# Recurrent scan of the second layer: first level on the keys themselves, sixteen-wide cells and the last distance moved to ScalarE

## What is computed

```python
log_f = jnp.logaddexp(jnp.log(lb), jnp.log1p(-lb) + jax.nn.log_sigmoid(f))
k = (1.0 - lb) * jax.nn.sigmoid(-f)
# per chunk, G = cumsum(log_f):
attn  = einsum('bhtk,bhsk,bhtsk->bhts', q, k, exp(G_t - G_s))   # s <= t
o     = einsum('bhts,bhsv->bhtv', attn, v) + einsum(q * exp(G), state)
```

## Time and profile before

| | us |
|---|---|
| median of 3 runs | 1880.17 |
| lowest, highest | 1879.79, 1880.75 |
| the profiled execution's own time | 1879.63 |
| its span in the profile | 1877.8 |
| PE busy | 1840.6 (98%) |
| DVE busy | 1147.7 (61%) |
| ACT busy | 938.7 (50%) |
| POOL busy | 588.5 (31%) |

### The profile page before, as it was taken

One profiled execution on the slowest core, in us unless ns is written; L12 is line 12 of the kernel. 1 busy time (PEld: TensorE's weight loads), 2 busy tenths in 40 slices (PEclk: granted clock), 3 DMA queues, 4 the chain that ended last, 5 costly groups with the idle time before them and its releaser, 6 DMA issues.

```text
span 1877.8 us, 25493 instructions
## 1 busy us (share of the span) xinstructions
PE 1840.6 (98%) x10128; PEld 1588.0 (85%) x10128; DVE 1147.7 (61%) x2028; ACT 938.7 (50%) x1107; POOL 588.5 (31%) x131
## 2 busy tenths in 40 slices
PE   8899999999998999999999999999999999999998
PEld 7688888888897988888888888899888889888887
DVE  7788878776888787222776322567522287862227
ACT  7455555455653554444554544453444455544443
POOL 2000000000000003888100888400588800058880
PEclk9899999999999999999999999999999999999999
DMA  9344444454243335655543555544655543365551
GB/s 360 112 159 156 143 164 152 180 196 155 93 166 131 120 128 195 215 191 192 187 181 136 181 194 189 188 190 165 227 199 192 190 177 135 112 233 199 193 190 65
DMA packets 53049, 325.56 MB, mean 173 GB/s; under 512 B 8624, under 2 KB 11056, under 8 KB 15568
## 3 DMA queue, kind: packets, MB, share of 16 engines
q1 hardware_dynamic: 45328, 310.49, 45.2%
q10 hardware_dynamic: 7616, 13.59, 2.1%
HBM read 323.02 MB, written 1.05 MB: 173 GB/s over the span
## 4 chain that ended last, share of the span: by engine, by line
PE 85%; DVE 10%; issue 2%; ACT 2%; DMA 1%; DVEq 0%; ACTq 0%
PE project L1102 31%; PE output L1102 31%; PE turn L1500 5%; PE project L1500 5%; PE project L1506 2%; PE turn L1506 2%; PE turn L1323 2%; DVE wlo L1962 2%; PE output L1288 1%; PE output L1263 1%; DVE arena L2302 1%; DMA raw<-in_units 1%; DVE arena L2079 1%; DVE arena L2325 1%; PE turn L1242 1%
## 5 line engine op out<-in xcount | busy, mean ns | idle before, releaser
L1059 POOL TENSOR_TENSOR wlo<-raw,whi 128x2048 fp32r<-128x2048 f32 x127 | 588.3, 4664 | 1240.8 <-ACT whi L1569 1224.1
L1569 ACT ACTIVATE whi<-raw 128x2048 fp32r<-128x2048 f32 x289 | 547.0, 1910 | 342.6 <-PE project L1500 166.2
L1102 PE MATMUL project<-whi,XT 128*128 128x512 f32 x1376 | 453.3, 400 | 11.4 <-ACT arena L1578 9.0
L1962 DVE TENSOR_TENSOR wlo<-raw,whi 128x2048 fp32r<-128x2048 f32 x162 | 368.3, 2285 | 23.1 <-ACT whi L1569 20.0
L1102 PEld LDWEIGHTS project<-whi,XT 128*128 128x128 f32 x1376 | 259.7, 189 | 67.0 <-ACT arena L1578 8.2
L1102 PE MATMUL output<-whi,YTh 128*128 128x512 f32 x736 | 288.1, 392 | 1.5 <-DVE YTl L2456 1.5
L1102 PE MATMUL output<-whi,YTl 128*128 128x512 f32 x736 | 287.1, 390 | 0.0
L1102 PE MATMUL output<-wlo,YTh 128*128 128x512 f32 x736 | 286.9, 390 | 0.0
L2740 DVE TENSOR_TENSOR arena<-project,arena 128x256 f32<-128x256 f32 x48 | 20.4, 425 | 409.1 <-ACT arena L1918 409.1
L1102 PE MATMUL project<-wlo,XT 128*128 128x512 f32 x688 | 268.9, 391 | 0.0
L1102 PE MATMUL project<-XT,whi 128*128 128x256 f32 x1184 | 219.0, 285 | 0.1
(11 more groups left out here) (283 smaller groups left out, 2386.8 us busy)
## 6 DMA issues: line engine op xcount, KB each, us to landing
raw<-in_units SPq DMA_DIRECT2D x290, 1024.0 KB, 4.8
arena<-in_ln_g ACTq DMA_DIRECT2D x8, 512.0 KB, 5.4
arena<-in_ln_b ACTq DMA_DIRECT2D x8, 512.0 KB, 7.3
raw<-in_units SPq DMA_DIRECT2D x2, 512.0 KB, 7.3
tok<-in_mem SPq DMA_DIRECT2D x1, 1024.0 KB, 14.4
arena<-in_x_t SPq DMA_DIRECT2D x1, 1024.0 KB, 18.2
xres<-in_x SPq DMA_DIRECT2D x1, 1024.0 KB, 20.1
arena<-in_mem_t ACTq DMA_DIRECT2D x1, 1024.0 KB, 4.5
```

The costliest lines, as they stand in the source:

```text
L1059: pool.tensor_tensor(wlo[:, slot, :], raw[:, slot, :], whi[:, slot, :], ALU.subtract).then_inc(lo_pool, 1)
L1102: mm = pe.matmul(out, x if x_stationary else w, w if x_stationary else x, start=start and i == 0, stop=stop and i == 2, skip_group_check=True)
L1569: act.activation(whi[:, slot, :], raw[:, slot, :], ACT.Copy).then_inc(hi_done, 1)
L1962: dve.tensor_tensor(wlo[:, slot, :], raw[:, slot, :], whi[:, slot, :], ALU.subtract).then_inc(lo_dve, 1)
```

## The change

It touches the two scans of the second layer alone; the GLA scans get their counts of `d_ready` shifted and are otherwise as before.
- Level 1: the left block is a single token, which is its own "mid", so its distance is 0 and its decay 1. The left distance (L2325) and the left product (L2308) are left out, ACT's exponential takes only the 512 right elements of each partition, and PE takes the keys from `kFB` itself.
- Level 5: its cells are taken over by ACT, in four copies of 16 partitions x 128 elements, in the place of DVE's predicated copy. By the order above they stand in ACT's step of level 6, behind the exponential of level 6.
- Level 8: DVE's left distance is left out. ACT takes it in its exponential, as scale -1 with the last column of the left half as a bias, in four instructions of 128 x 128; then follows the right exponential of 128 x 512. ACT waits for the products of level 6 in place of the distance.

```diff
         def scalar_evacuates(g, l):
-            return l in ((0, 6, 7, 8) if g else (6, 7, 8))
+            return l in ((0, 6, 7, 8) if g else (5, 6, 7, 8))
...
                     if l:
                         qf = QE[l % 2] if g else ZB[l % 2]
-                        kf = KE[l % 2] if g and l < 7 else qf
+                        kf = KE[l % 2] if g and l < 7 else kFB if l == 1 else qf
...
                     moves = [(AT[0:64, :, 0:2, 64:128], compact[0:64])]
+                elif l == 5:
+                    moves = [(AT[32 * n:32 * n + 16, :, 0:2, 32 * n + 16:32 * n + 32],
+                              compact[32 * n:32 * n + 16, :, :, 16 * n:16 * n + 16]) for n in range(4)]
...
                     if l:
-                        act.wait_ge(d_ready, 8 * (f["L"] // 9) + l)
+                        scan = f["L"] // 9
+                        if g:
+                            act.wait_ge(d_ready, 14 + 8 * (scan - 2) + l)
+                        elif l < 8:
+                            act.wait_ge(d_ready, 7 * scan + l)
+                        else:
+                            act.wait_ge(z_ready, f["L"] - 1)
                         Dx, s = decay_buffer(g, l), -1.0 / 16 if g else 1.0
-                        if l < 8:
+                        if l == 1 and not g:
+                            Dv = Dx.rearrange("p (n a) -> p n a", a=2)
+                            ins = act.activation(Dv[:, :, 1], Dv[:, :, 1], ACT.Exp)
+                        elif l < 8:
                             ins = act.activation(Dx, Dx, ACT.Exp, scale=s)
+                        elif not g:
+                            Dv, Gv = (x.rearrange("p (n a b) -> p n a b", a=2, b=P) for x in (Dx, GB))
+                            for n in range(4):
+                                act.activation(Dv[:, n, 0, :], Gv[:, n, 0, :], ACT.Exp, bias=Gv[:, n, 0, P - 1:P], scale=-1.0).then_inc(act_own, 1)
+                                last.own()
+                            ins = act.activation(Dv[:, :, 1, :], Gv[:, :, 1, :], ACT.Exp)
...
-                if l < 8:
+                if l < (8 if g else 7):
                     distances(g, l + 1)
...
                     Z = view(QE[l % 2] if g else ZB[l % 2])
-                    dve.tensor_tensor(Z[:, :, 1, :], view(q)[:, :, 1, :], view(Dx)[:, :, 1, :], ALU.mult).then_inc(dve_own, 1)
-                    last.own()
-                    dve.tensor_tensor(Z[:, :, 0, :], view(k)[:, :, 0, :], view(Dx)[:, :, 0, :], ALU.mult).then_inc(z_ready, 1)
+                    right = dve.tensor_tensor(Z[:, :, 1, :], view(q)[:, :, 1, :], view(Dx)[:, :, 1, :], ALU.mult)
+                    if l == 1:
+                        right.then_inc(z_ready, 1)
+                    else:
+                        right.then_inc(dve_own, 1)
+                        last.own()
+                        dve.tensor_tensor(Z[:, :, 0, :], view(k)[:, :, 0, :], view(Dx)[:, :, 0, :], ALU.mult).then_inc(z_ready, 1)
...
                 if l < 8:
-                    dve.tensor_tensor(Dv[:, :, 1, :], Gv[:, :, 1, :], mid, ALU.subtract).then_inc(dve_own, 1)
+                    right = dve.tensor_tensor(Dv[:, :, 1, :], Gv[:, :, 1, :], mid, ALU.subtract)
+                    if l == 1 and not g:
+                        right.then_inc(d_ready, 1)
+                        last.other(d_ready, nth("d"))
+                        return
+                    right.then_inc(dve_own, 1)
                     last.own()
```

## The result

| | before | after |
|---|---|---|
| median, 22 runs each | 1880.76 us | 1884.68 us |
| lowest | 1879.43 us | 1883.62 us |
| span of the profiled execution | 1877.8 us | 1882.5 us |

The ratio is 1.0025, with a 95% interval from 1.0018 to 1.0032: the change makes the kernel 4.7 us slower (3.4 to 6.0). The two medians are 3.9 us apart, which lies in that interval too. A difference of 0.2% (3.8 us) is about what a measurement of this kernel can tell from none: the 4.7 us lie above that, the lower end of the interval doesn't.

A forecast was written before the change was run, and what follows sets the result against it. PE, busy 98% of the span, was taken as the bound. Chain 2.60 + 1.44 us (level 1's gains counted) plus clock 0.7 made 4.7 us on 1879.63, or 1884.4; the median forecast was 1884.9 us, range 1881.0 to 1889.0.

The forecast's parts named there:

- the clock: PE at half speed over level 8 and the first eight matmuls on the values in both scans: 0.7 us more.
- What bounds: PE, busy 98% of the span, bounds the kernel; DVE or ACT changes count only through PE's idle time.
- Level 1: Dropped left distance and product shorten DVE's chain to level 2: gains of 0.27 and 0.60 us, 0.87 in sum.
- Level 5: ACT's four copies, 0.29 us each, wait for PE's level 5 and hold the tanhs and exponential 7 behind them.
- The chain: From PE's level 5 end to level 8: 2.87 and 2.04 us later, less level 1's gains 2.60 and 1.44.
- Level 8: ACT's exponential in five instructions, four at 0.305 us and one at 0.61: 1.83 us in place of 1.14.
- against the second: Rival, chance 0.12: PE's level 5 ends before ACT wants its copies, so ACT is never held; 1879.9 us, not slower.
- against the third: Rival, chance 0.05: each DVE instruction removed counts for PE, 5.1 us in all; 1875.1 us, faster.
- The clock did not stay down: Rival, chance 0.12: half speed over all 24 matmuls on the values in each scan; 8.3 us more, 1888.5 us.
- The cheap prices: Rival, chance 0.15: copies at 0.20 us, early gaps closed for 1.7 us, clock no worse; 2.5 us more, 1882.7 us.

The follow-up runs named there:

- x_filled2: Changed kernel plus 16 (first scan) and 12 (second) unread identity matmuls on PE ahead of its wait for level 7; 1884.72 us, ratio 1.0018.
- x_gate_filled: Kernel before with levels 1 and 8 changed, exponential 8 early, gate product between its weight splits, 5 filling matmuls ahead of level 7; 1875.36 us, ratio 0.9972.

## Why the prediction was right

1884.9 us was predicted, 1884.68 measured. The mechanism was the predicted one, and the starts of levels 7 and 8 came out to 0.2 us in each scan. That the time agrees to 0.2 us is luck: the clock was sized 1.0 us too small, the ratio's interval is 2.6 us wide, and the difference of the medians is 3.9 us, not 4.7. Step by step:

- **What bounds** was right: PE lost the time idling; its busy time grew by 1.0 us alone. The waits' own naming (DVE) would have misled, since DVE had less to do; what decided was the order of ACT's queue.
- **Level 1**: the end of level 5 comes 0.21 and 0.58 us earlier in the profile (0.27 and 0.60 predicted), counted from DVE's first distance in the first scan and from level 0 in the second. PE's wait before level 2 is gone in the first scan, as said; that before level 4 grew from 0.2 to 0.6 us, for the reason given, that DVE can't evacuate level 1 before PE has done it.
- **Level 5**: four copies in 1.17 us (510.83 to 512.00), 0.29 us each, for 0.29 taken from the 32 x 128 form. Half the partitions make it no cheaper. The estimate of 0.20 us worked out from the Trainium skill (ScalarE: Activation LUTs, under what ACT_TABLE_LOAD costs: back-to-back activations overlap by about 93 ns) did not hold, since these copies don't overlap: three of them last 0.85 us at 0.27 each.
- **The chain**: level 7 at 4.62 and 3.64 us (4.71 and 3.67 predicted), level 8 at 7.09 and 6.26 us (7.25 and 6.21). With level 1's gains that is 2.5 and 1.5 us, 4.0 in all, where 2.60 and 1.44 were predicted. The new wait of PE before level 8 was written down as 1 to 1.5 us and came out as 0.5 and 0.65 us: level 7 ran at half speed (1.97 us in both scans, 1.15 with the clock up) and took up the rest. With the clock filled up it was 1.3 us in the first scan.
- **Level 8**: the four pointer forms are 0.30 us apart (1.19 us to the next start at 515.89), all five 1.80 us, for 1.83.
- **The clock** was the term with the wrong size. Taken at 0.7 us, it was 1.7 us in this pair of profiles: from level 8 to the next dense work the first scan took 6.24 us for 4.89 before, the second 13.95 for 13.60. In the first scan it is the matmuls on the values that slowed, as written; in the second the first eight were as slow before (1.91 us in both), and it is level 8 and the matmuls behind the eight that slowed a little. Chain and clock make 5.7 us, which is what both scans take more. That the profiled span still grew by 4.7 us alone is because this execution reached the first scan a microsecond sooner (DVE's distance 1 at 481.71 us for 482.70), which has nothing to do with the change. Over many executions the clock's share can't be told: filling it away changed no median by more than the noise.
- **The rivals**: ACT was held, against the second. The freed DVE time was worth nothing with ACT's order as it stood, against the third; in another order, with level 5 left on DVE, three of its four instructions went (0.60 + 0.60 + 0.61 us a scan, 3.6 us in all), and the kernel was 4.5 us (2.4 to 6.6) faster. The clock did not stay down over all the matmuls on the values; it came back in the midst of them, at about 523.4 us in the first scan, where 5 of the 8 pairs of rows behind the first eight had been slow. The cheap prices were not there.

## What to carry to other kernels

An engine that works in order doesn't only pay for what is moved to it: everything behind the moved instruction waits for that instruction's input. Ask of each moved step what it waits for, when that comes, and what stands behind it in the new queue; an evacuation belongs behind the work whose inputs are already there, and even there it can cost something, as the copies ahead of exponential 8 did. When a wait names one engine, look whether that engine was itself waiting. Set two profiles against each other between two instructions that both have, and not by their spans: what differs elsewhere falls out. And once one chain is shortened, look for the next product that shares a queue with bulk work.

## What was not expected

- A half-speed stretch of PE that is filled away can come back at the next idle time: with the fillers of x_filled2 the clock was 1.00 at the ends of both scans, and another stretch stood at 606.5 us (598.6 us in x_gate_filled), with no gain in the median in either case.
- A float32 matmul of 128 x 128 by 128 columns appears as two matmuls of 0.12 us from start to start: 32 issued made 64 rows and 7.41 us.
- All these kernels do the same work up to the first scan, yet their profiled executions reach it up to 1.7 us apart (DVE's first distance at 481.39 to 483.10 us). Between before and the changed kernel the microsecond comes from one place: PE starts again at 55.46 and 55.27 us, after 7.73 and 7.63 us of idle time, at half speed, and comes back to full speed later before (granted clock 0.50 in 56 to 60 us and 0.86 in 60 to 64 us) than after (0.60 and 1.00). That sets a floor to what one profile of this kernel can tell by its span; distances inside a scan repeat to about 0.02 us where the clock is the same.
